# Loading tokens ahead of modulation tiles, and summing head squares by two rounded-type products, in a two-block transformer kernel

## What is computed

```python
m_l = (sc_lat @ w_ada[l] + b_ada[l])[:, None, :]          # modulation
hl = modulate(rmsnorm(lat, norm_g[l, 0]), sh1, sc1)       # h * (1 + scale) + shift
hc = modulate(rmsnorm(cx, norm_g[l, 0]), csh1, csc1)
q, zf_fwd, zf_bwd, v, g = jnp.split(h @ w_in, 5, axis=-1) # v first in this kernel
...
o = rmsnorm(o, g_gain)     # per head: mean of squares over the 128 value columns
return (o * jax.nn.silu(g)) @ w_out
...
return rmsnorm(lat, final_g)                              # end of the first block
```

## Time and profile before

| | |
|---|---|
| median of three runs | 875.71 us (875.36 to 875.9) |
| the profiled execution's own time | 874.96 us |
| its span, first to last instruction | 873.1 us |
| TensorE busy | 863.6 us, 99% of the span |
| VectorE busy | 641.5 us, 73% |
| ScalarE busy | 488.5 us, 56% |
| DMA | 160.90 MB, mean 184 GB/s |

### The profile page before, as it was taken

The page is one execution under the profiler, slowest core; times in us unless marked ns, Lnnn a source line. Parts: engine busy times, 40 slices in busy tenths (PEclk is TensorE's granted clock), DMA queues, the critical chain, the costliest instruction groups (busy, mean ns, idle before and its releaser), DMA issues.

```text
span 873.1 us, 16932 instructions
## 1 busy us (share of the span) xinstructions
PE 863.6 (99%) x6308; PEld 783.7 (90%) x6308; DVE 641.5 (73%) x1080; ACT 488.5 (56%) x769; POOL 0.2 (0%) x4
## 2 busy tenths in 40 slices
PE   8999999999999999999999999999999999999997
PEld 3688888888899999999998899999998899999996
DVE  3793899999997787877677897766577765555555
ACT  5433677777766664655557545555544664444443
POOL 0000000000000000000000000000000000000000
PEclk9999999999999999999999999999999999999999
DMA  9974444444447556565564654444465465555551
GB/s 343 408 285 158 145 146 146 143 144 144 160 143 252 185 202 242 170 216 186 175 191 143 196 193 146 150 165 146 145 218 171 140 200 195 185 192 185 180 188 48
DMA packets 45585, 160.90 MB, mean 184 GB/s; under 512 B 5216, under 2 KB 6624, under 8 KB 45408
## 3 DMA queue, kind: packets, MB, share of 16 engines
q1 hardware_dynamic: 43632, 156.43, 52.7%
q10 hardware_dynamic: 1904, 3.81, 1.3%
HBM read 159.16 MB, written 1.05 MB: 183 GB/s over the span
## 4 chain that ended last, share of the span: by engine, by line
PE 94%; DVE 2%; ACT 1%; DMA 1%; SPq 0%; issue 0%; DVEq 0%; ACTq 0%
PE bank L420 22%; PE bank L422 21%; PE bank L421 21%; PE bank L474 5%; PE bank L476 5%; PE bank L475 5%; PE bank L1224 2%; PE bank L1227 2%; PE bank L1225 2%; DMA tok<-in_tok 1%; PE bank L442 1%; PE bank L1315 1%; PE bank L1333 1%; PE bank L1195 1%; PE bank L1296 0%; DVE arena L657 0%
## 5 line engine op out<-in xcount | busy, mean ns | idle before, releaser
L414 DVE TENSOR_TENSOR w_lo<-raw,w_hi 128x1024 fp32r<-128x1024 f32 x244 | 295.2, 1223 | 118.0 <-ACT w_hi L407 117.9
L420 PE MATMUL bank<-h_hi,w_hi 128*128 128x256 f32 (+1 forms) x1168 | 350.1, 300 | 0.0
L422 PE MATMUL bank<-h_hi,w_lo 128*128 128x256 f32 (+1 forms) x1168 | 343.5, 294 | 0.0
L421 PE MATMUL bank<-h_lo,w_hi 128*128 128x256 f32 (+1 forms) x1168 | 343.4, 294 | 0.0
L407 ACT ACTIVATE w_hi<-raw 128x1024 fp32r<-128x1024 f32 x244 | 252.7, 1051 | 111.3 <-PE bank L422 82.9
L420 PEld LDWEIGHTS bank<-h_hi,w_hi 128*128 128x128 f32 x1168 | 219.5, 188 | 9.5 <-issue 0.8
L421 PEld LDWEIGHTS bank<-h_lo,w_hi 128*128 128x128 f32 x1168 | 220.3, 189 | 6.5
L422 PEld LDWEIGHTS bank<-h_hi,w_lo 128*128 128x128 f32 x1168 | 220.0, 188 | 5.8
L420 PE MATMUL bank<-y_hi,w_hi 128*128 128x256 f32 x304 | 87.0, 286 | 0.1
L421 PE MATMUL bank<-y_lo,w_hi 128*128 128x256 f32 x304 | 85.6, 282 | 0.0
L422 PE MATMUL bank<-y_hi,w_lo 128*128 128x256 f32 x304 | 85.5, 281 | 0.0
(11 more groups left out here) (272 smaller groups left out, 1100.5 us busy)
## 6 DMA issues: line engine op xcount, KB each, us to landing
raw<-in_stream SPq DMA_DIRECT2D x244, 512.0 KB, 3.4
arena<-in_ada SPq DMA_DIRECT2D x40, 512.0 KB, 7.2
xres<-in_ada SPq DMA_DIRECT2D x8, 512.0 KB, 3.3
tok<-in_tok SPq DMA_DIRECT2D x3, 512.0 KB, 7.7
con<-in_con ACTq DMA_DIRECT2D x1, 1472.0 KB, 7.1
xres<-in_tok ACTq DMA_DIRECT2D x1, 1024.0 KB, 10.1
out<-arena SPq DMA_DIRECT2D x4, 256.0 KB, 2.0
tok<-in_tok SPq DMA_DIRECT2D x2, 256.0 KB, 9.5
```

The costliest lines, as they stand in the source:

```text
L414: dve.tensor_tensor(w_lo[c.slot][:, :], raw[c.slot][:, :], w_hi[c.slot][:, :].bitcast(F32), ALU.subtract).then_inc(S("split_lo"), 1)
L420: pe.matmul(dst, hi_w, a_hi, start=start, stop=False, skip_group_check=True)
L421: pe.matmul(dst, hi_w, a_lo, start=False, stop=False, skip_group_check=True)
L422: return pe.matmul(dst, lo_w, a_hi, start=False, stop=stop, skip_group_check=True)
```

## The change

It has three parts.

1. In the opening all tokens, in four pieces of two column tiles, are loaded ahead of modulation tiles 0 to 3. TensorE sums all tokens first, then multiplies tiles 0 to 3, transposes, makes four products on zeros (before: 6, 1 and 2 at three places), and starts the values. Tile 4 is multiplied with 5 to 7, behind all four token tiles of k = 0 (before: behind two of them, with tile 4 done ahead). The first two pairs of token tiles take all products with `w_hi` first, then those with `w_lo`. `value_tiles` waits for `split_hi` and `split_lo` at each tile. VectorE norms k = 0 to 3 in whole tiles ahead of quarter 0, and makes `w_lo` of chunk 1 ahead of quarter 1.
2. In the loop over heads, the sum of squares is made of two fp32r products (`ones_r` with the high and the low part of the squares) in place of one fp32 product. ScalarE makes one more square, `o_sq_hi`; VectorE makes `o_sq_lo`, behind `scale_qk`. The sum stands behind the sixth k-step of the column tile, not the fourth. `ones_r` is copied once. The last two heads keep the fp32 sum.
3. In the chunks `N_IN2`, one `hi` moves between the first four and the last four squares, and the `lo` move to suit.

```diff
-            load_ada(0)
-            load_ada(1)
-            load_tokens(0)
-            load_ada(2)
-            load_tokens(1)
-            load_tokens(2)
-            load_ada(3)
-            load_tokens(3)
-            load_tokens(4)
+            for n in range(4):
+                load_tokens(n)
+            for i in range(4):
+                load_ada(i)
             load_one(0)
...
+            def value_tiles(j, b, tiles):
...
+                pe.wait_ge(S("split_hi"), c.n + 1)
+                for tile in tiles:
+                    dst, x = part(tile)
+                    pe.wait_ge(S("h_hi"), 2 * k + 1 + tile // 2)
+                    pe.matmul(dst, h_hi[:, x], hi_w, start=k == 0, stop=False, skip_group_check=True)
+                pe.wait_ge(S("split_lo"), c.n + 1)
+                for tile in tiles:
+                    dst, x = part(tile)
+                    pe.matmul(dst, h_hi[:, x], lo_w, start=False, stop=False, skip_group_check=True)
+                for tile in tiles:
+                    dst, x = part(tile)
+                    pe.wait_ge(S("h_lo"), 2 * k + 1 + tile // 2)
+                    last = pe.matmul(dst, h_lo[:, x], hi_w, start=False, stop=k == KT - 1, skip_group_check=True)
...
+            value_tiles(0, 0, [0, 1])
+            value_tiles(0, 0, [2, 3])
+            ada(4, 8)
+            value_tiles(0, 1, [0])
+            value_tiles(0, 1, [1])
+            turn_rows(1)
+            value_tiles(0, 1, [2])
+            value_tiles(0, 1, [3]).then_inc(S("multiplied"), 1)
...
-            def out_squares(h):
+            def out_squares(h, count):
                 act.wait_ge(S("o"), h + 1)
+                if count == 2:
+                    act.activation(o_sq_hi, o_bank, ACT.Square).then_inc(S("o_squares"), 1)
                 act.activation(o_sq, o_bank, ACT.Square).then_inc(S("o_squares"), 1)
...
+            def out_sum_split(h, dst):
+                pe.wait_ge(S("o_squares"), h * 3 + 3)
+                pe.matmul(dst, ones_r, o_sq_hi, start=True, stop=False, skip_group_check=True)
+                pe.matmul(dst, ones_r, o_sq_lo, start=False, stop=True, skip_group_check=True).then_inc(S("o_summed"), 1)
...
-                column_tile(pe, at(1), psum[1][:, :], TC, TC, halfway=last_sum if prev2 else None)
+                column_tile(pe, at(1), psum[1][:, :], TC, TC, last_sum if prev2 else None, KT - 3)
...
                     scale_qk(h - 1, 1 - u)
+                if prev2:
+                    dve.wait_ge(S("o_squares"), h * 3 - 4)
+                    dve.tensor_tensor(o_sq_lo, o_sq, o_sq_hi.bitcast(F32), ALU.subtract).then_inc(S("o_squares"), 1)
                 lo(dve, at(AHEAD))
...
-            square_residual(act, 1)
-            for k in range(2, 6):
+            square_residual(act, 1, 0, KT // 2)
+            hi(act, Chunk(N_IN2, 2 + AHEAD))
+            square_residual(act, 1, KT // 2)
+            for k in range(3, 6):
                 hi(act, Chunk(N_IN2, k + AHEAD))
```

More of the change, by code:

```diff
@@ L292, in build @@
         o_sq = part(T)
+        ones_r = y_hi[:, (KT - 2) * T:(KT - 2) * T + P]
+        o_sq_hi, o_sq_lo = (y[:, (KT - 1) * T:KT * T] for y in (y_hi, y_lo))
         o_rs = part(T)
@@ L429, in column_tile @@
                              h_lo[:, k * width:k * width + n_tok], k == 0, k == KT - 1)
-                if halfway is not None and k == KT // 2 - 1:
-                    halfway()
+                if between is not None and k == behind:
+                    between()
             last.then_inc(S("multiplied"), 1)
@@ L531, in wait_residual, with square_residual @@
             engine.wait_ge(S("residual"), update * KT + m + 1)
-        def square_residual(act, update):
-            for m in range(KT):
+        def square_residual(act, update, first=0, end=KT):
+            for m in range(first, end):
                 wait_residual(act, update, m)
@@ L1211, in turn_rows, with part @@
                 last.then_inc(S("mod_turned"), 1)
+            def value_tiles(j, b, tiles):
+                c, half = Chunk(j), j // 4
+                k = 2 * (j % 4) + b
+                hi_w, lo_w = (w[c.slot][:, b * 512:b * 512 + 512] for w in (w_hi, w_lo))
+                def part(tile):
+                    return psum[4 * half + tile][:, :], slice(k * TC + tile * P, k * TC + (tile + 1) * P)
+                pe.wait_ge(S("split_hi"), c.n + 1)
[11 more added lines that the diff above has]
+                    last = pe.matmul(dst, h_lo[:, x], hi_w, start=False, stop=k == KT - 1, skip_group_check=True)
+                    if k == KT - 1 and tile < 3:
+                        last.then_inc(S("v_bank"), 1)
+                return last
@@ L1213, in values @@
             def values(j, between={}):
-                c, half = Chunk(j), j // 4
-                pe.wait_ge(S("split_lo"), c.n + 1)
                 for b in range(2):
-                    k = 2 * (j % 4) + b
                     for tile in range(4):
-                        x = slice(k * TC + tile * P, k * TC + (tile + 1) * P)
-                        dst = psum[4 * half + tile][:, :]
-                        hi_w, lo_w = (w[c.slot][:, b * 512:b * 512 + 512] for w in (w_hi, w_lo))
-                        pe.wait_ge(S("h_hi"), 2 * k + 1 + tile // 2)
-                        pe.matmul(dst, h_hi[:, x], hi_w, start=k == 0, stop=False, skip_group_check=True)
-                        pe.matmul(dst, h_hi[:, x], lo_w, start=False, stop=False, skip_group_check=True)
-                        pe.wait_ge(S("h_lo"), 2 * k + 1 + tile // 2)
-                        last = pe.matmul(dst, h_lo[:, x], hi_w, start=False, stop=k == KT - 1, skip_group_check=True)
-                        if k == KT - 1 and tile < 3:
-                            last.then_inc(S("v_bank"), 1)
+                        last = value_tiles(j, b, [tile])
@@ L1759, in _ @@
                 dve.tensor_tensor(x, x, wide[:, (k + 1) * TC:(k + 2) * TC], ALU.add).then_inc(S("tok_added"), 1)
+            dve.wait_ge(S("tok_rstd"), 4)
+            for k in range(4):
+                norm_tokens(k)
             dve.wait_ge(S("par_in"), 16)
```

91 lines of the change are left out of this document (34 added, 57 removed).

## The result

| | before | after |
|---|---|---|
| median of seven runs on the same chip | 875.56 us (875.00 to 876.03) | 877.48 us (877.11 to 878.91) |
| the profiled execution's own time | 874.96 us | 877.4 us |
| its span | 873.1 us | 875.6 us |

The ratio after to before is 1.0025, with a 95% interval of 1.0015 to 1.0035: the changed kernel is 0.25% slower. Forecast were 878.0 us (874.8 to 880.0) and slower by over 0.2%.

A forecast was written before the change was run, and what follows sets the result against it. TensorE, busy 99% of the span, was taken to bound the kernel. Opening +0.5, heads +1.9 and chunks `N_IN2` -0.05 gave +2.3 on 874.96, so 877.3, and 878.0 us for the median, range 874.8 to 880.0.

The forecast's parts named there:

- Part 2, the mechanism: Heads: VectorE's subtraction stands behind `scale_qk`, ends at 165.69, and TensorE waits 0.5 us for it at the new sum.
- the prediction's answer "No": Heads: the wait doesn't heal from head to head, since VectorE's work starts again from TensorE's clock each time.
- Part 2, the sizes: Each head costs 0.50 wait + 0.24 pair - 0.43 fp32 sum = +0.31; six heads +1.9 us, bounds -1.15 to +3.1.
- Part 2, what is late next: Heads, before column tile 2: gated output ready at 168.0, needed at about 169.1, 0.7 us of cover; sigmoids under 1 us late.
- Part 1: Opening: values start 0.96 us earlier, but TensorE waits a microsecond ahead of k = 2; +0.5 us, bounds -0.96 to +1.0.
- the sum of the chain, 28.48: Opening: links from modulation tile 3's landing at 14.89 through quarter 1 and `h_hi` put k = 2 at 28.48, before 28.05.
- Part 3: Chunks `N_IN2`: the moved `hi` removes the late step of 0.29 instead of 0.235 near 481 us; -0.05 us.
- The sum: Whole kernel: 0.5 + 1.9 - 0.05 = +2.3 on the profiled 874.96, 877.3; plus 0.75 for the median, 878.0.
- The difference isn't late: Heads: VectorE's subtraction ends by 165.15, TensorE doesn't wait, each head gains 0.19; -0.7, 875.0 us; chance 0.16.
- The lead is kept: Opening: quarter 1 is ready before TensorE has done k = 1; heads as forecast; +0.9, 876.6 us; chance 0.11.
- The clock: Opening: the clock falls while TensorE has only single tiles between 13.5 and 17.4 us; 881.7 us; chance 0.05.
- The wait in the heads grows: Heads: gated output late too, 0.7 cover gone and 0.3 more in each head; +1.8, 879.8 us; chance 0.08.

The follow-up runs named there:

- opening_only: Changed kernel with the old fp32 sum of squares and old end of the block, so only the opening is changed: 875.41 us (0.9988 to 1.0006).
- heads_only: Kernel before with the change to the heads alone (two fp32r products behind the sixth k-step, low part behind `scale_qk`): 877.73 us (1.0015 to 1.0033).
- low_on_pool: Kernel before with the change to the heads alone, but GpSimd makes the low part of the squares instead of VectorE: 874.54 us (0.9977 to 0.9996).
- end_only: Kernel before with the third part of the change alone (one `hi` moved between the squares in chunks `N_IN2`): 875.33 us, one run.
- all_mended: Changed kernel with the low part made within `scale_qk` and VectorE's states added between the two late rows: 874.19 us, ratio 0.9983 (0.9974 to 0.9992).
- heads_sum7: Kernel before with the change to the heads alone, but the two fp32r products stand behind the seventh k-step: 875.09 us (0.9985 to 1.0003).

## Why the prediction was right, and where not

- **Part 2, the mechanism: right, and shown.** The difference comes behind the end of `scale_qk`, and TensorE waits for it in all six heads, 0.365 to 0.475 us, 0.41 in the mean, where 0.5 was reckoned. Taking it earlier or asking for it later removes the wait, and putting it later lengthens it one for one. That it doesn't heal (the prediction's answer "No") was right.
- **Part 2, the sizes.** 0.31 was forecast for a head, 0.50 + 0.24 - 0.43; measured is 0.32, 0.41 + 0.34 - 0.43. Two terms were off by about 0.1 each and cancel, so that the sum fits so well is luck. The wait: VectorE's low part ended 0.395 behind the place of the sum, as reckoned (0.39), but TensorE started 0.05 to 0.06 behind its end in all six heads, where I had taken 0.14 to 0.16 from a row of ScalarE; and every second wait was shorter by another 0.1 (0.365 against 0.445 to 0.475). The pair: I took the 0.12 step of a dense stream for a product that stands behind a wait, where it is 0.22. Without the wait the 0.24 was exact. The six heads gave +1.94 where +1.9 was forecast, and with what follows +2.04.
- **Part 2, what is late next: the wrong place.** I named the gated output, with 0.7 us of cover. It never made TensorE wait. The late work showed at the states behind the last pass, with 0.45 us of cover, which I hadn't looked at, since I read one head inside the loop and took it for all six. It cost 0.38 us there, and 0.28 came back by the last outputs, since the kernel before had a wait of its own at the sum of head 6. The step that I mis-sized is the sigmoids, put at less than 1 us: they start 2.05 us ahead of column tile 2 in the head shown of the kernel before (166.76, 168.81) and 0.65 ahead in the changed one (169.28, 169.93), 1.4 later against a tile that is itself later, and VectorE idles 0.51 us for them there.
- **Part 1: wrong, +0.5 forecast.** The order of events was right (lead, wait of 0.8 to 1 us ahead of k = 2, released by `h_hi`). The step that failed is the sum of the chain, 28.48. From tile 3 on, each link came earlier: first product 18.68 for 18.96, end of group 2 at 23.87 for 24.2, quarter 1 at 26.65 for 27.1, k = 2 at 28.09. Most of it is there at the first link: tile 3 is multiplied from 14.67, and I had put its landing at 14.89, the end of a token load in the old order. The rest is that rows next to each other on one engine overlap by some 0.1 us, which I counted in full. Moreover the yardstick was one profile: with the old opening, group 3 starts anywhere from 29.38 to 30.23 in nine profiles (29.92 in the middle), with the new one from 29.59 to 29.85 in four. The 29.55 of the kernel before is thus an early one, and against the middle of the nine the changed kernel's 29.65 is 0.3 ahead, not 0.1 behind. The opening can't be held against a single start to 0.5 us; the time of opening_only (0.9988 to 1.0006) shows no effect, to within -1.1 and +0.5 us.
- **Part 3: right** (the step of 0.29 goes, 0.05 us).
- **The sum.** +2.3 was forecast, +2.05 is measured at the MLP's loop, where the profile stands; the medians differ by 1.92. Two errors partly cancel: the opening was 0.4 too high, the heads with what follows 0.14 too low. The 0.75 that I added from the profile to the median was 0.08 in the changed kernel (877.4 and 877.48).
- **The rivals.** "The difference isn't late" fell with the wait in all six heads. "The lead is kept" fell: k = 2 starts at 28.09. The clock did not fall: it is 1.00 in each five microseconds of the first 40 in the changed kernel, so what the Trainium skill says (TensorE: Matmul & The Clock Gate, "What's actually happening"), that an array which has been idle runs at half rate, did not come into play there. "The wait in the heads grows" fell for the gated output.

## What to carry to other kernels

A product that is made cheaper on a full engine is worth its saving only if its new operand is ready, so look first at where the instruction that makes it stands on its own engine: 0.34 us of VectorE in the wrong place cost 0.5 us of TensorE in each head, and eight small instructions earlier it cost nothing there. Read the last pass of a loop apart from the others, since what follows it can be due a whole tile earlier, and ask for the cover there. And hold a gain of a few tenths of a microsecond against several profiles or by starts within one stage: a start behind the first loads of a kernel moved by 0.85 us between profiles of kernels whose opening is the same.

## What the runs showed of the hardware that I had not expected

**The first product behind a wait** holds up the next by 0.22 us, where in the dense stream it is 0.12 (durations 384 against 281 ns). So a short wait cost 0.10 more than it lasted, in all six heads of the changed kernel and of heads_only.

**VectorE's small two-input rows behind a GpSimd row** (low_on_pool) took 0.90 us a pair in place of 0.35, six times out of six.

**Two spacings of the same products.** In the MLP's loop the products are the same in all kernels here. From its first product to the last it takes 175.22 us in the profile of before and 175.59 in that of after:

```profile
692.22 0.28 PE L420 MATMUL bank<-h_hi,w_hi 128*128 128x256 f32 x1
...
867.44 0.39 PE L476 MATMUL bank<-w_hi,y_lo 128*128 128x512 f32 x1
```

```profile
694.27 0.28 PE L417 MATMUL bank<-h_hi,w_hi 128*128 128x256 f32 x1
...
869.86 0.40 PE L473 MATMUL bank<-w_hi,y_lo 128*128 128x512 f32 x1
```

Of thirteen profiles four (before, heads_only, end_only and all_mended) have 175.21 or 175.22, and nine have 175.59 or 175.60; nothing lies between, there is no wait, and the 0.38 is spread evenly over the loop. It goes with none of the edits: heads_only has the short one and heads_sum7 the long one. So 0.37 of the 2.42 us between the two profiles are not the change. Whether it goes with the execution or with how a program lies in memory stays open.
